# The entry of a two-layer trunk: the first layer starts from x times (1 + scale), and the normalising root and the shift are put on after the product

## The reference

```python
def ada_modulation(c, w, b):
    mod = jax.nn.silu(c) @ w + b
    shift, scale, gate = jnp.split(mod[:, None, :], 3, axis=-1)
...
h = rms_norm(x) * (1.0 + scale) + shift
...
proj = h @ w_in                      # first sub-layer: forgetting attention
q, k, v, f_logit = jnp.split(proj, [1024, 2048, 3072], axis=-1)
log_f = jax.nn.log_sigmoid(f_logit + b_f)
cum = jnp.cumsum(log_f, axis=1)
s = q @ k.T * scale + (cum_q - cum_k)     # per head, causal, then softmax, times v
```

## Time and profile before

| | us |
|---|---|
| median of 3 runs | 1294.53 (1294.26 to 1295.54) |
| profiled execution, its own time | 1294.75 |
| profiled execution, its span | 1293.0 |
| PE busy | 1255.4 (97%) |
| DVE busy | 858.0 (66%) |
| ACT busy | 546.5 (42%) |

### The profile page before, as it was taken

How to read it: one execution, slowest core, us unless ns; L and a number is a source line. 1 busy time by engine, 2 the same in 40 slices (tenths; PEclk the granted TensorE clock), 3 DMA queues, 4 the chain that set the end, 5 groups by cost and what they waited for, 6 DMA issues and landing times.

```text
span 1293.0 us, 17963 instructions
## 1 busy us (share of the span) xinstructions
PE 1255.4 (97%) x6173; PEld 983.4 (76%) x6173; DVE 858.0 (66%) x1302; ACT 546.5 (42%) x996; POOL 41.6 (3%) x47
## 2 busy tenths in 40 slices
PE   5999999999999999999999999999999999999997
PEld 3677777668788878788888666667788888888886
DVE  2657666758988888855548777765876666663332
ACT  5543444444533333322234566664543333332222
POOL 2000000003000000000020000000300000000000
PEclk7999999999999999999999999999999999999998
DMA  9624334332556656556532111123233333333332
GB/s 309 193 66 130 121 126 131 111 102 82 163 189 193 194 190 196 161 186 192 166 94 61 40 31 41 30 60 98 67 113 95 94 94 95 95 93 104 90 91 93
DMA packets 241013, 154.43 MB, mean 119 GB/s; under 512 B 38153, under 2 KB 232174, under 8 KB 237882
## 3 DMA queue, kind: packets, MB, share of 16 engines
q1 hardware_dynamic: 240954, 153.63, 39.9%
HBM read 151.47 MB, written 2.14 MB: 119 GB/s over the span
## 4 chain that ended last, share of the span: by engine, by line
PE 84%; DVE 8%; ACT 3%; SPq 2%; issue 2%; DMA 1%; POOL 0%; DVEq 0%; ACTq 0%; POOLq 0%
PE pj L1692 71%; PE ov L1946 3%; PE sc L1890 3%; PE tr L1918 2%; DVE wl L1128 2%; PE sc L1902 1%; SPq L529 1%; ACT wh L711 1%; DVE ada_w_sb L1169 1%; DVE tmp L1245 1%; ACT tmp L855 1%; DMA first_ada<-in_ada_w_dram 1%; DVE nmax L1314 1%; PE ov L1831 0%; DVE hl L1226 0%
## 5 line engine op out<-in xcount | busy, mean ns | idle before, releaser
L1128 DVE TENSOR_TENSOR wl<-raw,wh 128x1024 fp32r<-128x1024 f32 (+2 forms) x214 | 237.7, 1111 | 246.9 <-ACT wh L711 243.0
L711 ACT ACTIVATE wh<-raw 128x1024 fp32r<-128x1024 f32 (+2 forms) x214 | 204.4, 955 | 441.4 <-PE pj L1692 438.1
L1692 PE MATMUL pj<-hh,wh 128*128 128x512 f32 x928 | 370.2, 399 | 3.8 <-issue 2.7
L1692 PE MATMUL pj<-hh,wl 128*128 128x512 f32 x928 | 362.1, 390 | 0.0
L1692 PE MATMUL pj<-hl,wh 128*128 128x512 f32 x928 | 361.4, 389 | 0.0
L1692 PE MATMUL pj<-gh,wh 128*128 128x512 f32 x576 | 229.0, 398 | 1.1 <-DVE rope_sb L1614 0.5
L1692 PE MATMUL pj<-gh,wl 128*128 128x512 f32 x576 | 225.1, 391 | 0.0
L1692 PE MATMUL pj<-gl,wh 128*128 128x512 f32 x576 | 224.8, 390 | 0.0
L1692 PEld LDWEIGHTS pj<-hh,wh 128*128 128x128 f32 x928 | 174.3, 188 | 43.9 <-issue 9.7
L1692 PEld LDWEIGHTS pj<-hh,wl 128*128 128x128 f32 x928 | 174.2, 188 | 37.2
L1692 PEld LDWEIGHTS pj<-hl,wh 128*128 128x128 f32 x928 | 174.6, 188 | 33.0
(11 more groups left out here) (214 smaller groups left out, 1134.6 us busy)
## 6 DMA issues: line engine op xcount, KB each, us to landing
raw<-in_ffn_w_in_dram SPq DMA_DIRECT2D x88, 512.0 KB, 3.9
ada_w_sb<-in_ada_w_dram SPq DMA_DIRECT2D x40, 1024.0 KB, 5.1
raw<-in_ffn_w_out_dram SPq DMA_DIRECT2D x32, 448.0 KB, 3.5
raw<-in_fox_w_in_dram SPq DMA_DIRECT2D x24, 512.0 KB, 3.9
first_ada<-in_ada_w_dram SPq DMA_DIRECT2D x16, 512.0 KB, 9.0
raw<-in_ffn_w_out_dram SPq DMA_DIRECT2D x16, 512.0 KB, 3.6
raw<-in_fox_w_o_dram SPq DMA_DIRECT2D x8, 512.0 KB, 3.8
raw<-in_mla_w_o_dram SPq DMA_DIRECT2D x8, 512.0 KB, 3.7
```

The lines of the kernel that those rows point to most:

```text
L711: act.activation(wh[:, n0 % 2, 0:kt, :], raw[:, n0 % 2, 0:kt, :], ACT.Copy).then_inc(w_hi, 1)
L1128: dve.tensor_tensor(wl[:, n0 % 2, 0:kt, :], raw[:, n0 % 2, 0:kt, :], f32(wh[:, n0 % 2, 0:kt, :]), ALU.subtract).then_inc(w_lo, 1)
L1692: ins = pe.matmul(bank_[:, :], (wl if term == 2 else wh)[:, s, kt, :], (rl if term == 1 else rh)(kt), start=start and j == 0, stop=stop an ...
```

## The change

The 2048 columns are loaded in five blocks: scale first, in 256, 256 and 512 columns, then shift in 512 and 512. As soon as a block of scale is turned, ScalarE and VectorE make `u = x * (1 + scale)` in high and low part (`first_high`, `first_lows`), and TensorE multiplies q, the gate logits and k from u. The root is put on their results by VectorE (`z_scaled` and the product with `rb_sb`), and the shift is added: `f_shift_sum` and 16 `first_shift` matmuls of one column multiply the shift into the unsplit weights. v is still made from h. The squares are made half by ScalarE and half by VectorE and are no longer added up first: TensorE takes each of the eight tiles with four matmuls of one column (`first_square`), with one 512-column matmul after each but the last whose result nobody reads. `turn_block` takes one matmul for each 128 columns. The square-root table is loaded before x is taken, and an exponential one after `first_high(3)`. SP loads the q weights behind block 0 and the k weights behind block 2, into places of their own; the convolution weights wait for the last block's row, the second modulation load for `f_shift`.

```diff
-BLOCKS = 4
-BW = D // BLOCKS
-BT = BW // P
+FIRST = ((D, 2 * P), (D + 2 * P, 2 * P), (D + 4 * P, 4 * P), (0, 4 * P), (4 * P, 4 * P))
+BLOCKS = len(FIRST)
+FIRST_SCALES = 3
...
+            def first_weight(j):
+
+                sp.dma_start(raw_tile(j), fox[:, j * D:j * D + P].rearrange("(t p) n -> p t n", p=P)
+                             ).then_inc(first_in[j], 16)
+
             for b in range(BLOCKS):
+                c0, n = FIRST[b]
                 for h in range(2):
                     k0 = h * (DT // 2)
-                    for side in range(2):
-                        c0 = side * D + b * BW
-                        sp.dma_start(first_w[:, b, k0:k0 + DT // 2, side, :],
-                                     ada_w[0, 0][k0 * P:(k0 + DT // 2) * P, c0:c0 + BW].rearrange(
-                                         "(t p) n -> p t n", p=P)).then_inc(ada0_in[b], 16)
-                if b == 1:
+                    sp.dma_start(first_w(b)[:, k0:k0 + DT // 2, :],
+                                 ada_w[0, 0][k0 * P:(k0 + DT // 2) * P, c0:c0 + n].rearrange("(t p) n -> p t n", p=P)
+                                 ).then_inc(ada0_in[b][h], 16)
+                if b == 0:
+                    first_weight(0)
+                if b == 2:
                     sp.dma_start(f_raw[:, :, :], fox[:, 3 * D:3 * D + HEADS].rearrange("(t p) n -> p t n", p=P)
                                  ).then_inc(f_in, 16)
-                    load(C_FOX, DT, fox[:, 0:P])
-            load(C_FOX + 1, DT, fox[:, D:D + P])
+                    first_weight(1)
+            load(C_FOX + 2, DT, fox[:, 2 * D:2 * D + P])
+            load(C_FOX + 3, DT, fox[:, P:2 * P])
             sp.dma_start(bf_sb[:, :], fox_b_f.rearrange("l h -> h l")).then_inc(rest_in, 16)
             sp.wait_ge(x_t, 2 * QB)
             ada_load(0)
-            load(C_FOX + 2, DT, fox[:, 2 * D:2 * D + P])
+            sp.wait_ge(block_row, BLOCKS)
...
+            block_take(0)
+            split(C_FOX)
             norm(0)
-            for b in range(2):
-                block_take(b)
+            act.wait_ge(block_ok, 1)
+            first_high(0)
+            first_high(1)
+            act.wait_ge(rb, 1)
+            act.activation(rb_sb, OV[1][:, :], ACT.Copy).then_inc(rb_copy, 1)
+            block_take(1)
+            act.wait_ge(block_ok, 2)
+            first_high(2)
+            first_high(3)
+            act.activation(early[:, 7:8], eps[:, 0:1], ACT.Exp)
             act.wait_ge(f_in, 16)
             act.activation(f_wh[:, :, :], f_raw[:, :, :], ACT.Copy).then_inc(f_hi, 1)
-            split(C_FOX)
-            act.wait_ge(block_ok, 1)
-            high(0, 0)
-            high(0, 1)
-            act.wait_ge(block_ok, 2)
-            high(0, 2)
             block_take(2)
-            high(0, 3)
+            split(C_FOX + 1)
             act.wait_ge(block_ok, 3)
-            high(0, 4)
-            high(0, 5)
+            for kt in range(4, DT):
+                first_high(kt)
             block_take(3)
+            first_z(0)
             act.wait_ge(block_ok, 4)
-            high(0, 6)
-            high(0, 7)
-            split(C_FOX + 1)
-
-            act.wait_ge(fg_d, 2)
-            act.activation(fga[2], fga[0], ACT.Abs).then_inc(fg_a, 1)
+            for kt in range(4):
+                high(0, kt)
+            block_take(4)
+            split(C_FOX + 2)
+            act.wait_ge(block_ok, 5)
+            for kt in range(4, DT):
+                if kt == DT - 2:
+                    act.wait_ge(f_bias_s, 1)
+                    act.wait_ge(fg_d, 1)
+                    act.activation(fga[2], fga[0], ACT.Abs, bias=f_bias[:, 0:1]).then_inc(fg_a, 1)
+                high(0, kt)
+            first_z(1)
 
...
-            dve.memset(ssq[:, :], 0.0).then_inc(ssq_s, 1)
-            for kt in range(DT):
-                dve.wait_ge(sq, kt + 1)
-                dve.wait_ge(ssq_s, kt + 1)
-                dve.tensor_tensor(ssq[:, :], ssq[:, :], sqb[kt % 2], ALU.add).then_inc(ssq_s, 1)
-            norm(0)
+            def first_square(kt):
+
+                if kt == DT - 1:
+                    dve.wait_ge(sq_used, FIRST_SQ.index(4) + 1)
+                dve.tensor_tensor(first_sq[kt], xT[:, kt, :], xT[:, kt, :], ALU.mult).then_inc(sq_v, 1)
...
+            def first_lows(kts):
+
+                for kt in kts:
+                    dve.wait_ge(first_hi, kt + 1)
+                    dve.scalar_tensor_tensor(out=first_u(kt, False), in0=xT[:, kt, :], scalar=mod[:, 0, DT + kt:DT + kt + 1],
+                                             in1=f32(first_u(kt, True)), op0=ALU.mult, op1=ALU.subtract
+                                             ).then_inc(first_lo, 1)
...
+                for kt in kts:
+                    dve.scalar_tensor_tensor(out=first_pre(kt), in0=xT[:, kt, :], scalar=mod[:, 0, DT + kt:DT + kt + 1],
+                                             in1=OV[1][:, :], op0=ALU.mult, op1=ALU.mult).then_inc(pre, 1)
+
...
+
+                dve.wait_ge(z_t, j + 1)
+                dve.tensor_tensor(z_tile(j), z_tile(j), OV[1][:, :], ALU.mult).then_inc(z_s, 1)
+
+            def h_lows(kts):
+
+                for kt in kts:
+                    dve.wait_ge(h_hi, kt + 1)
+                    dve.scalar_tensor_tensor(out=h_tile(0, kt, False), in0=first_pre(kt), scalar=mod[:, 0, kt:kt + 1],
...
+
+            dve.wait_ge(x_e, 2 * QB)
+            for kt in range(4, DT):
+                first_square(kt)
             dve.wait_ge(consts, 6)
             dve.tensor_tensor(pick[:, :], ident[:, 0:P:HD], ident[:, HD // 2:P:HD], ALU.add).then_inc(pick_ok, 1)
-            block_shift_scale(0)
+            dve.wait_ge(pick_ok, 1)
+            dve.tensor_tensor(pick_all[:, :], pick[:, 0:1], pick[:, 1:2], ALU.add).then_inc(pick_ok, 1)
+            block_mod(0)
+            split(C_FOX)
+            norm(0)
+            dve.wait_ge(block_ok, 1)
+            first_lows((0, 1))
+            block_mod(1)
+            dve.wait_ge(block_ok, 2)
+            first_lows((2, 3))
+            dve.wait_ge(rb, 1)
+            first_pres((0, 1))
             dve.wait_ge(f_hi, 1)
             dve.tensor_tensor(f_wl[:, :, :], f_raw[:, :, :], f32(f_wh[:, :, :]), ALU.subtract).then_inc(f_lo, 1)
-            split(C_FOX)
-            modulated(0, 0)
-            dve.memset(fga[5], 1.0).then_inc(fg_d, 1)
+            block_mod(2)
             split(C_FOX + 1)
+            dve.wait_ge(block_ok, 3)
+            first_lows(range(4, DT))
+            first_pres(range(2, DT - 1))
+            block_mod(3)
+            z_scaled(0)
             dve.wait_ge(f_mm, 1)
+            dve.wait_ge(rb_copy, 1)
+            dve.tensor_tensor(fga[0], F_PSUM[0:HEADS, :], rb_sb[0:HEADS, :], ALU.mult).then_inc(fg_d, 1)
+            first_pres((DT - 1,))
+            dve.wait_ge(block_ok, 4)
+            h_lows(range(4))
+            split(C_FOX + 2)
+            block_mod(4)
+            dve.wait_ge(block_ok, 5)
             dve.wait_ge(rest_in, 16)
-            dve.tensor_scalar(fga[0], F_PSUM[0:HEADS, :], bf_sb[:, 0:1], None, ALU.add).then_inc(fg_d, 1)
-            dve.wait_ge(fg_d, 2)
-            dve.tensor_scalar(fga[1], fga[0], 0.0, None, ALU.min).then_inc(fg_d, 1)
+            dve.wait_ge(f_shift, 1)
+            dve.tensor_tensor(f_bias[:, :], SC[1][0:HEADS, 0:1], bf_sb[:, :], ALU.add).then_inc(f_bias_s, 1)
+            dve.wait_ge(f_bias_s, 1)
+            dve.wait_ge(fg_d, 1)
+            dve.tensor_scalar(fga[1], fga[0], f_bias[:, 0:1], 0.0, ALU.add, ALU.min).then_inc(fg_d, 1)
+            h_lows(range(4, DT))
+            z_scaled(1)
...
+                    for q in range(4):
+                        ins = pe.matmul(block_psum(b)[32 * q:32 * q + 1, :], csil[:, k0 + q:k0 + q + 1],
+                                        first_w(b)[:, k0 + q, :], start=k0 == 0, stop=k0 == DT - 4)
                 ins.then_inc(block_row, 1)
 
             def turn_block(b):
 
                 pe.wait_ge(block_sb, b + 1)
                 if b >= 2:
-                    pe.wait_ge(block_pre, b - 1)
-                for j in range(BT):
-                    ins = pe.matmul(block_turned(b)[:, j:j + BT + 1:BT], block_row_sb(b)[:, j * P:(j + 1) * P], pick[:, :],
+                    pe.wait_ge(block_ok, b - 1)
+                for j in range(FIRST[b][1] // P):
+                    ins = pe.matmul(block_turned(b)[:, j:j + 1], row_w[:, j * P:(j + 1) * P], pick_all[:, :],
                                     start=True, stop=True)
                 ins.then_inc(block_cols, 1)
...
-                                    (h_l if term == 1 else h_h)(kt), start=kt == 0 and term == 0,
+                                    (first_u_l if term == 1 else first_u_h)(kt), start=kt == 0 and term == 0,
                                     stop=kt == DT - 1 and term == 2)
                 if kt == DT - 1:
                     ins.then_inc(f_mm, 1)
 
-            def q_product(kt):
```

(96 more changed lines are left out.)

200 lines of the change are left out of this document (112 added, 88 removed).

## The result

| | before | after |
|---|---|---|
| median, us | 1295.03 (1294.26 to 1296.36) | 1314.87 (1313.78 to 1315.59) |
| profiled execution: its own time, its span | 1294.75, 1293.0 | 1314.38, 1312.6 |
| first score starts | 60.64 | 81.14 |
| PE busy | 1255.4 | 1277.2 |

The ratio is 1.0149, 95% interval 1.0136 to 1.0162: 19.8 us slower. The prediction was 1312.6, inside its own range but 2.3 us too low. The first score is 20.5 us later (forecast 17.9), and the span 19.6: 0.9 is given back later, nearly all of it before 905.05, where GpSimd starts an instruction that comes at 924.62 in after, 19.57 later. What gives it back is open.

The account below looks back on a forecast made before the run. TensorE, busy 97% of the span, was taken as the bound: first score at 77.6, 17.0 us later, plus 0.9 for a late level. 1293.0 + 17.9 + 1.75 = 1312.6; range 1299.5 to 1317, own case 1309 to 1316.

Parts of the forecast that it names:

- No transfer bounds the new entry: Entry: first result needs 1 MiB instead of 2 MiB, the last block is wanted past 50, so transfers bound nothing.
- TensorE's own work decides: Entry: 14.4 us added on TensorE; all its work from 14.5 ends at 62.3 without waits, later than 60.64.
- The lower level in the squares: Squares phase from about 14.5: one-column matmuls keep TensorE at 1.2 GHz throughout, 1.79 us a set.
- The two stretches of the earlier trace: 20.8 to 25.0 and from 1281.6: TensorE busy with many one-column matmuls, yet at 0.50 during or after.
- The rule of the Trainium skill: Squares: the level follows how busy TensorE is, so upper level, score 5.9 later, 1300.6; chance 0.16.
- Rival 2: Squares, turns, shifts: long narrow runs go faster, deciding at 0.068 us a record; no loss, 1293.3; chance 0.05.
- Squares and idle matmuls: Entry from 14.5: squares 14.3, idle ones 3.2, `block_rows(0)` 1.7 at the lower level, to 33.7.
- VectorE's split ahead of the reciprocal: Before `spread(0)`: a 1.2 us split ahead of the reciprocal holds TensorE's queue, a gap of about 1.6 us.
- From there to the score: From 39.3 to the first score: products, modulation, turns, shifts, `taps` and waits, 38.3, plus 0.9 for a late level.
- Waits of VectorE: Products: TensorE waits 1.0 at tile 2, 0.8 at tile 4, 0.2 at `block_mod(4)`, 0.3 for the copy into `cum`.
- The third rival: Entry: the chain of ScalarE and VectorE becomes the bound; scores wait 5 us or more, 1318; chance 0.07.
- After the first score: Behind the first score: the order of work is the old one; nothing moves by more than a microsecond.

Follow-up runs that it names:

- Experiment 9: 8 with block 4's row before k, q and k shifts in fours among k's last tiles and v, ScalarE's split and `cum` copy earlier: 1296.11, ratio 1.0012.
- experiment 1: The changed kernel without its seven idle 512-column matmuls: 1311.59, ratio to before 1.0123.
- experiment 5: The changed kernel with squares summed by 512-column float32 matmuls against ones, without `spread` and idle matmuls, reciprocal on 128x512: 1304.87, ratio 1.0068.
- experiment 2: The changed kernel with VectorE making block 0's scale behind the split of the q weights, not ahead of it: 1313.99, ratio 1.0138.
- Experiment 3: The changed kernel with the 16 q and k shift matmuls four at a time behind v's tiles 0 to 3: 1313.71, ratio 1.0144.
- 8: experiment 5 with squares rounded to fp32r, VectorE's reciprocal and root products behind later low parts, and two splits moved: 1298.43, ratio 1.0025.
- experiment 10: Experiment 9 with h's low parts and the v weights' split earlier, block 0's scale again ahead of the q weights' split: 1299.15, ratio 1.0033.
- 11: experiment 10 with the 128x512 reciprocal moved into VectorE's idle time before block 2: 1292.43, ratio 0.9970.
- experiment 4: The changed kernel with four idle 512-column matmuls between sets of squares instead of one: 1318.47, single executions 1311.32 to 1323.35, ratio 1.0158.

## Why the prediction came out right, step by step

- **No transfer bounds the new entry:** right. TensorE waits for none after 15.03.
- **TensorE's own work decides:** right. Even at the upper level I had it end at 62.3, later than before's score. Experiment 9 is the upper level throughout with squares of 2.3 us for 7.3 and no `spread` or idle matmuls, and still needs 59.93. Of its 45.9 us from the first square on, 4.2 are waits of TensorE (2.7 and 0.9 for VectorE, 0.6 for a transfer). Without them, and with the 7.5 us of squares, `spread` and idle matmuls back, the same work from 14.5 would end at 63.7 by this estimate, 3 behind before's score.
- **The lower level in the squares:** right, and a large part. The two stretches of the earlier trace rows named it; after shows the lower level from 16.05 to 39.94, with TensorE busy but for 1.45 us. The rule of the Trainium skill (TensorE: Matmul & The Clock Gate, "What's actually happening") that the level follows how busy TensorE is does not hold for such work: 8.10 busy of 8.10 at 0.50. Nor does it by experiment 1, and experiment 5 shows the same TensorE time in wide matmuls at 1.00. By that rule the time would have been 1300.6. Rival 2 wanted 0.068 us a record; the first set, still at the upper level, took 1.02/8 = 0.13.
- **Squares and idle matmuls:** 8 x 1.79 + 7 x 0.45 + 1.7 = 19.2 from 14.5, measured 17.95 from 15.03. A set with the idle matmul behind it costs 2.14, where I had 2.24, and the first went at the upper level (1.02). From the turn on it went the other way: `spread` took 2.08 and block 1's row 1.81, where I had 1.8 and 1.3. The 2.08 of `spread` stood in the earlier trace rows; I took the norm's 1.8 instead.
- **VectorE's split ahead of the reciprocal:** 1.6 forecast, 1.45 measured, 1.1 of it shown by experiment 2. The first product started at 39.19 (forecast 39.3). That this agrees to 0.1 is luck: a start 0.5 later, squares 1.2 shorter, and `spread` and row 0.8 longer cancel.
- **From there to the score:** forecast 38.3 and 0.9 for a late level, measured 41.95. Here lies all the error. v took 7.87 for 5.45 (+2.4) and the q and k shifts 4.41 for 3.65 (+0.8). The 48 products of q and k took 13.1 for 10.9 (+2.2): 0.57 of it is the first tile at the lower level, which the 0.9 was for, and the rest comes from tiles behind matmuls of another kind, which take 0.81 to 0.96 instead of 0.69. Against that stand the gate shift, 0.48 for 1.0 (-0.5), the turns, 2.7 for 3.2 (-0.5), and the waits, 1.7 for 2.3 (-0.6). The largest mis-sized term is v behind the shifts. I priced the 16 shift matmuls each by its own duration, though my argument on the squares was that such a run loses the level, and did not ask it of the shifts. Experiment 3 shows the cause: taken apart, they leave shifts and v at 1.00, and k's end to the first score is 2.4 shorter.
- **Waits of VectorE:** tile 2 waited 1.07 (forecast 1.0), tile 4 0.63 (forecast 0.8), the last copy into `cum` nothing, since TensorE was later: the copy ended at 77.57, 3.6 ahead of the first score. The third rival, though, ended last by 1.3 us in experiment 3, and became the bound as soon as TensorE's work was cut (8, 9, 10).
- **After the first score** the order is the same; 0.9 us was given back, within the 1 us that I had allowed; I had forecast none of it.

What stays open: why the level falls again in experiment 3 behind the short wait, and for a short while in the wide squares of experiment 10 but not in those of 9 and 11; what brings the later falls; and in which executions of experiment 4 the level came back. How the level would have stood in the squares with other data or a later start was not tried.

## What to carry to other kernels

A wait that is removed by moving work forward is only worth what TensorE doesn't have to do in its place: add up all of TensorE's work to the end of the stage first. Then ask of every run of one-column matmuls what it does to the granted clock of the wide ones behind it; make it wide where a 512-column matmul gives the same sum, or scatter it in fours. Before a difference of 1 to 2 us is put down to an edit, compare the traces stage by stage from a point that the edit does not reach, and look whether the level fell at other places. And a cheap helper instruction that is made 128 times wider must be priced again on its own engine and put where that engine is idle.

## What the runs showed of the hardware

- TensorE's level did not follow its busy share. In one-column float32 matmuls it stayed at 1.2 GHz through the squares of after (16.05 to 32.98), TensorE being busy 8.10 of 8.10 us from 24.80 to 32.90; the same squares as 512-column float32 matmuls (experiment 5, 3.67 us for four tiles) had 2.4 GHz. With 1.92 of each 3.42 us in 512-column matmuls it stayed at 1.2 GHz in one execution (experiment 4), while others of the same kernel were up to 12 us shorter. In after's shifts it fell from 2.4 GHz within 32 such records; eight of them between three wide matmuls did not bring it down (experiment 3, 1.00 from 66.60 to 77.10).
- Executions of one kernel differ in how long they have the lower level: mean granted clocks of 0.988 to 0.996 in experiment 10, with times from 1295.17 to 1304.44. A fall between 860 and 883 us cost 1.1.
- A 128x512 VectorE reciprocal took 3.27 to 3.35 us, where a product or difference of the same size takes 0.75, and the one of four columns 0.17 to 0.18.
- Idle matmuls cost 0.64 us each at the lower level between narrow ones, and shortened the set behind them from 1.73 to 1.50.
